# The first modulation in eight small tiles, each with its own chunk of weights, at the head of a two-layer backbone step

## The reference

```
mod = silu(cond) @ w_mod[l] + b_mod[l]          # w_mod[l]: 2048 x 6144 -> shift, scale, gate
xn  = rmsnorm(x, norm_w) * (1 + scale) + shift
P   = xn @ w_in[l]                              # cut into attention, convolution and GLA parts
A   = grouped-query attention with q/k norm and 2-D rotary   * silu(gate_A)
B   = Bg * conv3(Cg * h)                                     * silu(gate_B)
C   = two-way gated linear attention, scanned in chunks      * silu(gate_C)
x   = x + gate * concat(A, B, C) @ w_out[l]
```

## Time and profile before

| | us |
|---|---|
| median of three runs | 2141.55 |
| lowest and highest | 2139.41, 2141.57 |
| the profiled execution's own time | 2140.41 |
| its span in the trace | 2138.6 |
| TensorE busy | 2103.1 |
| VectorE busy | 1447.0 |
| ScalarE busy | 644.0 |

### The profile page before, as it was taken

One profiled execution on the slowest core, in us unless ns is written; L12 is line 12 of the kernel. 1 busy time (PEld: TensorE's weight loads), 2 busy tenths in 40 slices (PEclk: granted clock), 3 DMA queues, 4 the chain that ended last, 5 costly groups with the idle time before them and its releaser, 6 DMA issues.

```text
span 2138.6 us, 34996 instructions
## 1 busy us (share of the span) xinstructions
PE 2103.1 (98%) x13797; PEld 1894.9 (89%) x13797; DVE 1447.0 (68%) x2819; ACT 644.0 (30%) x1092; POOL 178.5 (8%) x118
## 2 busy tenths in 40 slices
PE   5999999999999999999999999999999999999998
PEld 4788887888999999999998888888799999999998
DVE  5869899999666656775465454566666566677654
ACT  4232221321333324442142222232133333353312
POOL 0000000000000000533310000000000000043321
PEclk9999999999999999999999999999999999999999
DMA  9989787675323324554435546454333233366443
GB/s 368 387 298 324 224 280 239 224 236 173 115 91 103 106 75 153 181 200 149 120 118 175 158 145 204 133 152 153 113 123 106 75 98 106 93 214 202 155 122 143
DMA packets 357333, 365.42 MB, mean 171 GB/s; under 512 B 17670, under 2 KB 264156, under 8 KB 356572
## 3 DMA queue, kind: packets, MB, share of 16 engines
q1 hardware_dynamic: 328528, 320.67, 46.8%
q10 hardware_dynamic: 28684, 43.09, 5.4%
HBM read 304.98 MB, written 58.72 MB: 170 GB/s over the span
## 4 chain that ended last, share of the span: by engine, by line
PE 95%; DMA 1%; DVE 1%; issue 1%; ACT 1%; ACTq 0%; SPq 0%; DVEq 0%
PE psP L885 31%; PE psP L959 20%; PE psP L980 11%; PE psT L897 8%; PE psO L1187 6%; PE psT L1187 4%; PE psO L1162 3%; PE psP L1116 3%; PE psT L1127 2%; PE psO L927 1%; PE psT L802 1%; PE psO L998 1%; PE psP L1199 1%; PE psP L914 0%; DMA wmod<-in_w_mod_dram 0%
## 5 line engine op out<-in xcount | busy, mean ns | idle before, releaser
L1883 DVE SCALAR_TENSOR_TENSOR macc<-mraw,cond,macc 128x384 f32<-128x384 f32 (+1 forms) x960 | 389.0, 476 | 0.0
L885 PE MATMUL psP<-x_high,high 128*128 128x512 f32 x852 | 337.2, 396 | 0.0
L885 PE MATMUL psP<-x_low,high 128*128 128x512 f32 x852 | 331.9, 390 | 0.0
L885 PE MATMUL psP<-x_high,low 128*128 128x512 f32 x852 | 331.7, 389 | 0.0
L1377 ACT ACTIVATE high<-raw 128x1024 fp32r<-128x1024 f32 x128 | 135.4, 1059 | 602.6 <-PE psT L897 494.9
L959 PE MATMUL psP<-x_high,high 128*128 128x320 f32 x1024 | 242.8, 318 | 0.0
L959 PE MATMUL psP<-x_high,low 128*128 128x320 f32 x1024 | 233.4, 309 | 0.0
L959 PE MATMUL psP<-x_low,high 128*128 128x320 f32 x1024 | 232.9, 309 | 0.0
L1901 DVE TENSOR_TENSOR low<-raw,high 128x1024 fp32r<-128x1024 f32 x128 | 156.4, 1223 | 71.3 <-ACT high L1377 71.3
L885 PEld LDWEIGHTS psP<-x_high,high 128*128 128x128 f32 x852 | 159.9, 188 | 39.7 <-issue 6.7
L885 PEld LDWEIGHTS psP<-x_low,high 128*128 128x128 f32 x852 | 159.9, 188 | 33.9
(11 more groups left out here) (332 smaller groups left out, 3784.3 us busy)
## 6 DMA issues: line engine op xcount, KB each, us to landing
raw<-in_w_in_dram SPq DMA_DIRECT2D x132, 512.0 KB, 5.9
wmod<-in_w_mod_dram SPq DMA_DIRECT2D x32, 1024.0 KB, 9.1
mraw<-in_w_mod_dram SPq DMA_DIRECT2D x64, 512.0 KB, 4.4
mraw<-in_w_mod_dram SPq DMA_DIRECT2D x32, 1024.0 KB, 7.1
raw<-in_w_in_dram SPq DMA_DIRECT2D x32, 1024.0 KB, 5.7
raw<-in_w_out_dram SPq DMA_DIRECT2D x64, 512.0 KB, 4.1
old<-x_scratch SPq DMA_DIRECT2D x64, 320.0 KB, 3.0
xf<-proj_scratch SPq DMA_DIRECT2D x48, 320.0 KB, 3.7
```

What stands on the lines that cost most here:

```text
L885: mm = pe.matmul(latent_ps[m], own, moved, start=(k == 0 and w is whole and x is x_high), stop=(k == KT - 1 and x is x_low))
L1883: m = dve.scalar_tensor_tensor(acc[:, v, 0:width], mraw[hf][:, k, 0:width], c, acc[:, v, 0:width], ALU.mult, ALU.add)
```

## The change

- The first modulation still has eight tiles of 512 columns, but each tile now holds 256 shift columns and the 256 scale columns that go with them. So each tile alone completes two k, a block is two k, and there are eight blocks in place of four. Each quarter is loaded by two transfers of 512 KB with rows of 1 KB, where it was one of 1 MB with rows of 2 KB.
- The first eight chunks of `w_in` are wide: 2 k by 768 columns, the extra columns with them, in two slots. The load order of tile t is quarter 0, 1, 2, chunk t, quarter 3.
- x is turned in 20 units (one token tile by four k), each token pair as soon as it has landed, ahead of the wait on the small rows; VectorE copies 20 times 512 columns.
- TensorE does tile 0 alone ahead of the first products. Behind its quarter 2 stand 24 products of the identity with itself (`keep_busy(24)`), behind its quarter 3 eight more; their result is not read.
- For tiles 2 to 7, VectorE sums quarter 0 of each; before, it was two quarters of three tiles. Again TensorE does 26 quarters; it adds VectorE's sums six times in place of three.
- ScalarE writes `x_high` itself and then `stage`, both from `x_hat`; VectorE's rounding step goes, and `x_low` is made apart for latent and prompt columns.
- VectorE scales the first four k ahead of the first flip, and the other twelve behind the first block's `x_low`.
- `quarters_after(t)` says ahead of which piece of block t the quarters of tile t+1 stand.

```diff
...
-PIECES_AFTER, PIECES_LAST = [0, 2, 1, 2, 1, 2, 1, 2], 3
-FIRST_QUARTERS = (3, 6, 8, 11)
...
+EXTRA_T = 2
+WIDE_T = GROUP_T + EXTRA_T
+WIDE_SLOTS = 2
+X_UNITS = TT * 4
+SCALED_FIRST = 2 * BLOCK_K
+def quarters_after(t):
+    if t == 0:
+        return {GROUP_T: (0, 1, 2), GROUP_T + 1: (3,)}
+    return {2: (1,), GROUP_T: (2,), GROUP_T + 1: (3,)}
+SUMMED_Q = 1
...
+            def mod_block(t, q):
+                sp.wait_ge(s[f"wmod_used{q}"], t + SEED)
+                for h in range(2):
+                    sp.dma_start(wmod[q][:, :, h * MOD_W:(h + 1) * MOD_W],
+                                 wm[:, q * QUARTER_K:(q + 1) * QUARTER_K, h * D + t * MOD_W:h * D + (t + 1) * MOD_W])\
...
+            for t in range(BLOCKS):
+                for q in range(3):
+                    mod_block(t, q)
+                front_chunk(0, t)
+                mod_block(t, 3)
+            for n in range(CHUNKS, CHUNKS + WIDE_SLOTS):
+                front_chunk(0, n)
...
+            def keep_busy(count):
+                for _ in range(count):
+                    pe.matmul(psT[:, 0:P], ident[:], ident[:], start=True, stop=True)
+            for u in range(X_UNITS):
+                i, q = u // 4, u % 4
+                if q == 0 and i % 2 == 0:
+                    pe.wait_ge(s[f"x_in{i // 2}"], 16 * min(2, TT - i))
+                if u >= len(start_banks):
+                    pe.wait_ge(s["x_taken"], u - len(start_banks) + 1)
+                for k in range(4):
+                    mm = pe.transpose(start_banks[u % len(start_banks)][:, k * P:(k + 1) * P],
+                                      xtok[:, i, (4 * q + k) * P:(4 * q + k + 1) * P], ident[:])
+                mm.then_inc(s["embed_turned"], 1)
             pe.wait_ge(s["rows_in"], 16 * 7 * DEPTH)
             for l in range(DEPTH):
-                pe.transpose(psP[l][:, 0:ROWS], rows[l][0:ROWS, :], ident[0:ROWS, 0:ROWS]).then_inc(s["rows_turned"], 1)
+                pe.transpose(rows_ps[l], rows[l][0:ROWS, :], ident[0:ROWS, 0:ROWS]).then_inc(s["rows_turned"], 1)
             pe.wait_ge(s["head_ready"], 2)
             pe.wait_ge(s["ones_set"], 2)
-            pe.wait_ge(s["x_in"], 16 * TT)
+            mod_quarter(0, 0)
+            mod_quarter(0, 1)
+            pe.wait_ge(s["stat_rs"], 3)
+            for i in range(TT):
+                mm = pe.matmul(rstd_ps[:, i * P:(i + 1) * P], x_rs[:, i:i + 1].to_broadcast([P, P]), ident[:],
+                               start=True, stop=True)
+            mm.then_inc(s["stat_summed"], 1)
+            mod_quarter(0, 2)
             pe.wait_ge(s["head_ready"], 2 + DEPTH)
-            for k in range(KT):
-                if k >= 2:
-                    pe.wait_ge(s["x_taken"], k - 1)
-                for i in range(TT):
-                    mm = pe.transpose(psP[k % 2][:, i * P:(i + 1) * P], xtok[:, i, k * P:(k + 1) * P], ident[:])
-                mm.then_inc(s["embed_turned"], 1)
-                if k in FIRST_QUARTERS:
-                    mod_quarter(0, FIRST_QUARTERS.index(k))
-            pe.wait_ge(s["x_squared"], 2 * TT)
-            pe.matmul(rs_ps[0], ones[:], r_a[:, 0:DEC], start=True, stop=True)
-            pe.matmul(rs_ps[1], ones[:], r_a[:, DEC:TOK], start=True, stop=True).then_inc(s["stat_summed"], 1)
-            for q in range(4):
-                mod_quarter(1, q)
+            keep_busy(24)
+            mod_quarter(0, 3)
+            keep_busy(8)
...
+                    first_pieces(0, range(GROUP_T))
+                    for t in range(BLOCKS):
+                        for i in range(GROUP_T if t == 0 else 0, WIDE_T + 1):
+                            for q in quarters_after(t).get(i, ()) if t + 1 < BLOCKS else ():
+                                mod_quarter(t + 1, q)
+                            wide_piece(t, i)
...
+                    for t in range(BLOCKS):
+                        cast_chunk(t)
+                        act.wait_ge(s["mod_ready"], t + 1)
+                        act.wait_ge(s["scaled"], (t + 1) * BLOCK_K)
+                        for v, part in ((0, slice(0, DEC)), (1, slice(DEC, TOK))):
+                            for k in range(t * BLOCK_K, (t + 1) * BLOCK_K):
+                                shift, factor = mod[:, k, v:v + 1], mod_a[:, k, v:v + 1]
+                                act.activation(x_high[:, k, part], x_hat[:, k, part], ACT.Identity, bias=shift, scale=factor)\
+                                    .then_inc(s["x_high"], 1)
+                                if t > 0:
+                                    act.wait_ge(s[("x_split", "x_prompt")[v]], k - BLOCK_K + 1)
+                                act.activation(stage[k % 2][:, part], x_hat[:, k, part], ACT.Identity, bias=shift, scale=factor)\
+                                    .then_inc(s["shifted"], 1)
...
+            for u in range(X_UNITS):
+                i, q = u // 4, u % 4
+                dve.wait_ge(s["embed_turned"], u + 1)
+                dve.tensor_copy(xf[:, 4 * q:4 * q + 4, i * P:(i + 1) * P],
+                                start_banks[u % len(start_banks)].rearrange("p (a t) -> p a t", t=P)).then_inc(s["x_taken"], 1)
+            dve.wait_ge(s["x_squared"], TT)
+            dve.tensor_scalar(x_var[:], x_sq[:], 1.0 / D, EPS, ALU.mult, ALU.add).then_inc(s["stat_var"], 1)
+            refine(x_rs[:], x_var[:], x_r0[:], x_tmp[:], "stat_exp", 1, "stat_rs", 0).then_inc(s["stat_rs"], 1)
...
+                def first_low(k, v):
+                    part = (slice(0, DEC), slice(DEC, TOK))[v]
+                    dve.wait_ge(s["x_high"], x_turn(k, v) + 1)
+                    dve.wait_ge(s["shifted"], x_turn(k, v) + 1)
+                    dve.tensor_tensor(x_low[:, k, part], stage[k % 2][:, part], x_high[:, k, part].bitcast(F32),
+                                      ALU.subtract).then_inc(s[("x_split", "x_prompt")[v]], 1)
...
+                    for k in range(SCALED_FIRST):
+                        scale_x(k)
+                    chunk_low(0)
                     dve.wait_ge(s["head_ready"], 2 + DEPTH)
-                    scale_block(0)
-                    for j in range(BLOCKS):
-                        if j > 0:
-                            flip(2 * j)
-                            early_sums(2 * j + 1)
-                        flip(2 * j + 1)
-                        dve.wait_ge(s["mod_turned"], 2 * j + 2)
-                        mod_sum([(slice(j * BLOCK_K, (j + 1) * BLOCK_K), flipped(2 * j + 1)),
-                                 (slice(KT + j * BLOCK_K, KT + (j + 1) * BLOCK_K), flipped(2 * j))],
-                                2 * j + 2, j * BLOCK_K, BLOCK_K)
-                        chunk_low(BLOCK_C * j)
-                        for k in range(j * BLOCK_K, (j + 1) * BLOCK_K):
-                            split_x(k % 2, k // 2)
-                            if k % BLOCK_K == 1:
-                                chunk_low(BLOCK_C * j + 1)
-                        dve.wait_ge(s["chunk_cast"], extra_turn(j) + 1)
-                        dve.tensor_tensor(extra_slot(low), extra_slot(raw), extra_slot(high).bitcast(F32), ALU.subtract)\
-                            .then_inc(s["chunk_split"], 1)
-                        if j + 1 < BLOCKS:
-                            scale_block(j + 1)
+                    for t in range(BLOCKS):
+                        flip(t)
+                        dve.wait_ge(s["mod_turned"], t + 1)
+                        first = t * BLOCK_K
+                        mod_sum([(slice(first, first + BLOCK_K), flipped(t)[:, 0:BLOCK_K]),
+                                 (slice(KT + first, KT + first + BLOCK_K), flipped(t)[:, BLOCK_K:])], 2 * t + 2, first, BLOCK_K)
+                        for v in range(2):
+                            for k in range(first, first + BLOCK_K):
+                                first_low(k, v)
+                        for k in range(SCALED_FIRST, KT) if t == 0 else ():
+                            scale_x(k)
+                        if t + 1 < BLOCKS:
+                            if vector_sums(t + 1, 0):
+                                early_sums(t + 1)
+                            chunk_low(t + 1)
...
```

More of the change, by code:

```diff
@@ L1028, in last_sums @@
                 mm.then_inc(s["stat_summed"], 1)
-            def keep_busy(count):
-                for _ in range(count):
-                    pe.matmul(psT[:, 0:P], ident[:], ident[:], start=True, stop=True)
             for l in range(DEPTH):
@@ L1796, in flip @@
                 dve.transpose(mod_turn[t % 2], mod_ps).then_inc(s["mod_turned"], 1)
[L1798 removed]
             dve.wait_ge(s["stat_summed"], 1)
[L1800 to L1802 removed]
+            dve.tensor_copy(rstd[:], rstd_ps).then_inc(s["x_squared"], 1)
+            dve.wait_ge(s["x_squared"], TT + 1)
             def raw_before(slot, l):
```

272 lines of the change are left out of this document (91 added, 181 removed).

## The result

The changed kernel takes 2157.5 us (median; 2157.05 to 2157.96), the kernel before, measured beside it, 2140.48 us (2138.24 to 2141.57). The ratio is 1.0081, with a 95% interval of 1.0063 to 1.0098: it is slower by 17 us. The forecast was 11.3 us slower, 2152.5 us in a range of 2144 to 2161 us. The profiled execution took 2157.05 us with a span of 2155.2 us; it is the fastest of the four, 0.45 us under their median.

What follows compares the result with a forecast made beforehand. TensorE was taken as the bound, busy 2103.1 of 2138.6 us. The stage ending 10.4 us later plus 0.9 us of slow clock gave +11.3 us on 2140.4: 2151.7 us, 2152.5 us as a median, range 2144 to 2161 us.

Steps and rivals of the forecast that it cites:

- The start: Head up to TensorE's first product: first flip at 37.8 us, first product at 39.6 us, 6.9 us ahead of before.
- The filler: Products of the identity ahead of the first flip, claimed to set it, 2.0 us behind VectorE's ready time.
- Block 0: First block: scalings hold the second flip until F0 + 16.5 us; TensorE idles 4.1 us, starting block 1 at F0 + 19.7.
- The half clock behind it: Slow clock after TensorE's wait ahead of block 1: priced at 0 to 1.7 us, 0.9 taken.
- Blocks 2 to 7: Cycles of 15.05 us each, with two TensorE waits on `x_low` per block, 0.54 and 0.76 us.
- The low clock in the prologue: Rival: clock falls in TensorE's idle time ahead of the norm's products, slowing the filler; +3 us, 2155.5 us; chance 0.13.
- the sum's last: End of the stage at F0 + 120.3 = 158.1 us, against 147.67 us before: 10.4 us later.
- F0: Time of the first flip in the prologue: 37.8 us, with bounds of 35.8 to 41 us.
- the forecast's own bounds: Total of 2147 to 2159 us, from F0 at -2 to +3 us and the flip-to-`x_low` link at 3 us.
- the link from flip to `x_low`: In each block, 3.23 us from a flip to k0's `x_low` reaching TensorE, 0.5 us either way, six times: 3 us.
- The rival of DMA as the bound: Quarter loads in 1 KB rows exceed their slack; two us beyond gives +12 us, 2164 us; chance 0.08.

Runs made afterwards that it cites:

- e1: The changed kernel with VectorE's twelve scalings done two at the end of each block, not in one stretch; 2154.8 us.
- e5: The changed kernel with the next tile's quarters one piece earlier, so two of three stand ahead of pieces 1 and 2; 2153.2 us.
- e6: As e5, with quarter 1 also loaded ahead of quarter 0 from tile 2 on; 2150.5 us.
- e7: The changed kernel with each quarter loaded by one transfer with rows of 2 KB, so modulating wrong columns; 2157.3 us.
- e3: The changed kernel with 16 products of the identity behind quarter 2 in place of 24; 2154.7 us.
- e4: The changed kernel without any products of the identity ahead of the first products; 2154.5 us.
- e10: The edits of e9 plus the two edits of e6, on the changed kernel; 2137.9 us.
- e12: The changed kernel with x turned only when all five tiles have landed; 2165.8 us.
- e2: The changed kernel with ScalarE taking the first group's four latent tiles out of PSUM ahead of the cast of chunk 10; 2153.7 us.
- e8: The changed kernel with chunks 8 to 10 requested ahead of the other loads that follow the stage; 2155.9 us.
- e9: The changed kernel with the edits of e1, e2 and e3 together; 2143.9 us.
- e11: As e10, plus nine products of the identity ahead of the norm's products and the prompt's result taken early; 2137.3 us.

## Why the prediction was right, and where it was short

- **The start.** Forecast: flip at 37.8 and first product at 39.6 us; measured 36.92 and 38.69 us. The turning took 0.8 us less than the sum: the copies were through at 25.4 against 26.2 us. The prediction took TensorE's full pace there from a granted clock of 1.00, which is no evidence, since that column shows 1.00 in the slow stretch as well (last section); the pace rose all the same. The filler does end later than VectorE's ready time (33.09 + 1.75 = 34.84 us), by 2.1 us where 2.0 was said.
- **Block 0.** Second flip at the first + 16.1 us (forecast 16.5), block 1 at + 19.4 us (19.7), the idle time of TensorE ahead of it 3.8 us (4.1). e1 shows that the twelve scalings in one stretch make it. The half clock behind it costs 8 distances of 0.43 in place of 0.2267 us, 1.6 us: at the upper end of the 0 to 1.7 us given, where 0.9 was taken.
- **Blocks 2 to 7.** 72.73 to 147.58 us in five cycles is 14.97 us each, forecast 15.05. The two gaps in a block, from the last product to the next less its 0.2267 us, are 0.55 us each, 1.1 in all where 0.54 and 0.76 were forecast. e5 and e6 show their cause.
- **DMA.** No bound: e7 leaves the blocks as they are, TensorE has no wait for a quarter in the changed kernel, and e6 goes from flip to flip in 13.6 us with the same rows of 1 KB, where the changed kernel takes 14.95. The five waits in e5 show that it would be the next bound, once TensorE asks earlier.
- **The low clock in the prologue.** It did not come in the profiled execution of the changed kernel, and did in six of the experiments' twelve (e1, e3, e4, e7, e10, e12). It was priced at 3 us. e1 and e7 have the same TensorE instructions up to the first product and have it at 40.02 and 39.64 in place of 38.69 us: 1.3 and 0.95 us.
- **The step that failed** is the sum's last: the end of the stage at F0 + 120.3 = 158.1 us, taken as the start of chunk 8, with "from there the work is the same". The products do end there: chunk 7's last is issued at 157.66 us, so chunk 8 could begin at 157.9 us. It begins at 162.95 us, and behind the wait come 1.6 us of half clock: 5.1 + 1.6 = 6.7 us that no term had. The sum compared what TensorE has to do in the stage and never asked who must free the banks of chunk 8. Removing the extra products from the stage's end took away the cover of ScalarE's three results, and they are themselves queued behind a cast that waits for TensorE's last product. With it the account closes: 10.2 us later at the end of the products, 5.1 of wait and 1.6 of clock make 16.9, and `lr_w` shows 17.0 us. e2 takes 5.6 of these back, and e8 shows that 0.9 of the wait is the landing. For the end of the products the forecast was 11.3 us (10.4, and 0.9 for the half clock ahead of them), so there it was 1.1 us too high, mostly by F0. 6.7 us without a term, less these 1.1, are the 5.6 us by which the forecast was short.

That the range held the time is in part luck. The direction, and the waits in the blocks, came as the sum had them. But the forecast's own bounds reached to 2159 us by up to 3 us for a later F0 and 3 us for the link from flip to `x_low`. F0 came 0.9 us early and the link took 3.27 us for 3.23; the room was used up by a wait that was not in the sum. The rival of DMA as the bound, at 2164 us, lay outside the range and did not happen.

## What to carry to other kernels

A stage's end is not the last product of the stage: follow each engine over the boundary, and ask for the first instruction behind it which buffer it needs, who frees that, and what stands ahead of the freeing on its queue. Work moved ahead of a chain that two engines pass to each other needs products behind it: where a reorder takes the filler pieces from behind a hand-over, each hand-over becomes a wait, and here a wait of about 4 us cost 1.6 to 3.0 us more in clock. A single-edit experiment can look small (2 to 4 us of 17 in e1 to e5), while the edits together brought back 20 us. The three edits of e9 move `lr_w` by 2.0, 5.6 and 1.8 us when they stand alone, 9.3 us in all, and by 13.1 us together. Part of the difference is that e1 and e3 were profiled in executions with the low clock in the prologue, and that a gain ahead of a wait which stays (chunk 8, with its low clock) does not come through whole.

## What the runs showed of the hardware

- **The same pause, two clocks.** TensorE is idle for the same 2.2 us ahead of the norm's products, behind the same instructions, in the changed kernel and in e1. In 28 to 32 us the granted clock is 1.00 in one execution and 0.62 in the other (shown above for e1). Of the other profiled executions with this pause, e2, e5, e6, e8 and e9 had 1.00 in these 4 us, and e3 0.57, e4 0.63, e7 0.62 and e10 0.59; e12, which gets there 7 to 8 us later, fell too:

```profile
28.00:32.00 4.00, 4.00 (x58) 3.63 (x59) 2.69 (x4) 1.48 (x1) 0.00 (x0) 1.00 1.09 383
```

Where the nine products fill this gap, in e11, TensorE is busy throughout 24 to 28 us at 1.00:

```profile
24.00:28.00 4.00, 4.00 (x62) 3.60 (x51) 1.18 (x6) 1.96 (x5) 0.00 (x0) 1.00 1.06 394
```

The executions differed before the pause already. VectorE's copies are 0.86 us apart until the turning picks up its pace. Where that came at 16.27 us or later (changed kernel, e2, e5, e8, e9), the clock stayed up in the pause. Where it came at 14.68 us or earlier (e3, e4, e7, e10), it fell. At 15.45 us it stayed in e6, and at 15.46 us it fell in e1. That is an order seen in eleven executions and not a cause shown; no run sets this moment. A prediction made ahead of the run can only give such a term a chance.
- **The price of the low clock behind a wait varies as well.** From chunk 8 to `lr_w` the instructions of TensorE are the same. The kernel before, e9, e10 and e11, which have no long wait ahead of chunk 8, take 376.13 to 376.15 us. Behind a wait of 4.0 us e5, e7 and e8 take 377.86 to 377.90, e12 378.57 and e4 379.10 us: 1.7 to 3.0 us more.
- **Turning picked up its pace on its own.** VectorE's first copies stand 0.86 us apart, each after a wait for TensorE; from 16.27 us fifteen copies take 9.10 us, 0.61 us each. Nothing but transpositions ran on TensorE from 10.85 to 23.4 us. The granted clock was 1.00 in the slow stretch already, with 11 transpositions in 2 us, where 16 to 18 us has 18 at the same 1.00:

```profile
14.00:16.00 2.00, 2.00 (x11) 2.00 (x10) 1.68 (x3) 0.91 (x3) 0.00 (x0) 1.00 0.99 416
```

So that column alone did not show the slow start. The Trainium skill ("TensorE: Matmul & The Clock Gate", Part 4: PE-mode transpose) says that transposes do not count as busy for the clock gate; in these rows the pace rose while only transpositions ran.
- **Rows of 1 KB were free.** With rows of 2 KB for the same bytes (e7) the stage took 118.84 us from its first product to chunk 7's last one, against 118.97 us.
